# Reordering the preparation of a bidirectional RWKV-7 scan inside a hybrid encoder kernel

## The reference

```
h = rms_norm(x); P = h @ w_in        # columns: RWKV-7 | convolution | latent attention | gates
RWKV-7:  p = p + (0.5*(prev + next) - p) * mu
         decay = exp(-exp(-softplus(-(w0 + tanh(wd) @ w_up)) - 0.5))      # per direction
         icl   = sigmoid(a0 + ad @ a_up)                                  # per direction
         v     = v + (v_first - v) * sigmoid(v0 + (h @ v_down) @ v_up)    # second layer only
         kk    = normalized(k * k_k) per head;  k_dir = k * (1 + (icl - 1) * k_a)
         state = state * w_t + (state a_t) b_t^T + v_t k_t^T;  out_t = state r_t   # both directions
         o = layer_norm(out + reversed out); o += bonus(r, k_dir, v); y = (o * g) @ w_branch
conv:    u = val * sigmoid(gate); 31-tap depthwise convolution; silu(layer_norm(u)) @ w_branch
merge:   x += (sum over branches of sigmoid(gate_b) * y_b) @ w_o
```

## Time and profile before

| | |
|---|---|
| median of 3 runs | 1811.07 us (1809.88 to 1813.27) |
| profiled execution | 1806.79 us, of which the span from first to last instruction is 1805.1 us |
| mean granted PE clock | 0.946 |
| PE busy | 1633.4 us, 90% |
| DVE busy | 1235.8 us, 68% |
| ACT busy | 769.1 us, 43% |
| POOL busy | 92.4 us, 5% |
| DMA | 231.58 MB, mean 128 GB/s |

### The profile page before, as it was taken

How to read it: one execution, slowest core, us unless ns; L and a number is a source line. 1 busy time by engine, 2 the same in 40 slices (tenths; PEclk the granted TensorE clock), 3 DMA queues, 4 the chain that set the end, 5 groups by cost and what they waited for, 6 DMA issues and landing times.

```text
span 1805.1 us, 43648 instructions
## 1 busy us (share of the span) xinstructions
PE 1633.4 (90%) x17117; PEld 1507.3 (84%) x17117; DVE 1235.8 (68%) x1850; ACT 769.1 (43%) x1163; POOL 92.4 (5%) x112
## 2 busy tenths in 40 slices
PE   6999998868878889999999999988688788999999
PEld 6999986757868869999889988867588687899997
DVE  5677667897647556777666777678874665567766
ACT  5444553435232135544444446534342311355444
POOL 1000100001100001000000002000011000010000
PEclk9999998978979989999999999989689799999999
DMA  5755532222102025555556554222220121355555
GB/s 187 263 181 184 173 106 71 94 94 71 38 25 84 27 81 165 178 187 178 189 195 227 187 185 166 94 71 95 70 85 25 36 72 38 102 165 180 187 183 192
DMA packets 62927, 231.58 MB, mean 128 GB/s; under 512 B 7024, under 2 KB 8048, under 8 KB 61840
## 3 DMA queue, kind: packets, MB, share of 16 engines
q1 hardware_dynamic: 61488, 221.41, 36.4%
q0 software_dynamic: 1248, 7.46, 1.1%
HBM read 228.09 MB, written 1.05 MB: 127 GB/s over the span
## 4 chain that ended last, share of the span: by engine, by line
PE 70%; DVE 14%; issue 9%; ACT 5%; DMA 2%; DVEq 0%; ACTq 0%; SPq 0%; POOLq 0%
PE banks L538 14%; PE banks L540 13%; PE banks L539 13%; PE banks L605 9%; PE banks L606 5%; DVE wlo L1407 3%; PE banks L939 2%; DMA raw<-in_stream 2%; DVE cvx L1635 2%; PE banks L937 2%; PE banks L928 1%; PE banks L865 1%; ACT whi L1083 1%; DVE arena L1848 1%; ACT arena L1260 1%
## 5 line engine op out<-in xcount | busy, mean ns | idle before, releaser
L1407 DVE TENSOR_TENSOR wlo<-raw,whi 128x1024 fp32r<-128x1024 f32 x417 | 511.8, 1231 | 327.0 <-ACT whi L1083 325.8
L1083 ACT CAST whi<-raw 128x1024 fp32r<-128x1024 f32 x417 | 435.4, 1048 | 442.4 <-PE banks L540 296.7
L538 PE MATMUL banks<-hx,whi 128*128 128x256 f32 x1696 | 491.9, 290 | 52.5 <-DVE wlo L1407 19.5
L540 PE MATMUL banks<-hx,wlo 128*128 128x256 f32 x1696 | 486.8, 287 | 0.0
L539 PE MATMUL banks<-hx,whi 128*128 128x256 f32 x1696 | 486.7, 287 | 0.0
L538 PEld LDWEIGHTS banks<-hx,whi 128*128 128x128 f32 x1696 | 332.6, 196 | 58.9 <-issue 20.6
L539 PEld LDWEIGHTS banks<-hx,whi 128*128 128x128 f32 x1696 | 332.6, 196 | 0.2
L540 PEld LDWEIGHTS banks<-hx,wlo 128*128 128x128 f32 x1696 | 332.3, 196 | 0.0
L538 PE MATMUL banks<-h,whi 128*128 128x256 f32 x896 | 275.1, 307 | 29.4 <-ACT arena L1180 16.6
L539 PE MATMUL banks<-h,whi 128*128 128x256 f32 x896 | 263.6, 294 | 0.0
L540 PE MATMUL banks<-h,wlo 128*128 128x256 f32 x896 | 262.9, 293 | 0.0
(11 more groups left out here) (293 smaller groups left out, 1888.8 us busy)
## 6 DMA issues: line engine op xcount, KB each, us to landing
raw<-in_stream SPq DMA_DIRECT2D x417, 512.0 KB, 3.3
arena<-in_wuq POOLq DMA_DIRECT2D x2, 1152.0 KB, 11.0
lo_w<-in_lora POOLq DMA_DIRECT2D x2, 1024.0 KB, 7.6
arena<-in_wukv POOLq DMA_DIRECT2D x2, 1024.0 KB, 15.0
xT<-in_x SPq DMA_DIRECT2D x1, 1024.0 KB, 4.9
out<-xT SPq DMA_DIRECT2D x8, 128.0 KB, 3.5
consts<-in_cst SPq DMA_DIRECT2D x1, 642.5 KB, 8.4
vec_t<-in_vecs POOLq DMA_DIRECT2D x3, 113.0 KB, 4.1
```

What stands on the lines that cost most here:

```text
L538: TE.matmul(o, wh, hi, start=first, stop=False, **kw)
L540: return TE.matmul(o, wl, hi, start=False, stop=last, **kw)
L1083: SE.copy(whi[:, m % HL, :], raw[:, m % RAW, :]).then_inc(hi_ready, 1)
L1407: TT(wlo[:, m % HL, :], raw[:, m % RAW, :], whi[:, m % HL, :].bitcast(F), ALU.subtract)\
```

## The change

The change has these parts, in both layers:

1. Column mixing: ACT writes a second copy of each column, scaled by 1 - mu, beside the plain one; DVE then needs two instructions for a column and not three. Two tiny DVE instructions a layer make the scale vectors.
2. The key's squares are taken by ACT straight from k with scale k_k, ahead of the last attention output. The multiplication by k_k on DVE goes; it is done in one instruction with the spread inverse norm.
3. First preparation: key sums, then at once the low-rank products for decay and icl, then the value gate, then the spread inverse norm. DVE does the prefix sums first and kk and the values after; the b and k products come before the exponentials' results are used. The three kinds of turned copies wait each for its own input.
4. Of the taps, 4 instead of 3 come after each attention pair; the other 42 go into the first solve, 4 in each of the five levels and 22 behind them. The convolution's mean and variance go behind the first solve, and its tail (sigmoid, products, rounding) into the second direction.
5. The update of `vfirst` goes into the second direction's solve.
6. States: only the three chunks that are needed are computed, each in one bank of its own; the step from state to state is accumulated by PE on top of the local state, and one DVE instruction over 128 partitions takes the place of four over 64. The added outputs take two banks and two DVE additions in place of four.
7. The second direction's low-rank products, sigmoids, prefix sums and b and k products go into the first direction's state steps.
8. `FILL_R` is redistributed; its sum stays 192.

The core of the diff:

```diff
-FILL_R = {"key sums": 8, "key inverse": 8, "values": 8}
+FILL_R = {"key sums": 6, "decay": 8, "nu": 5, "values": 5}
 for _d in range(2):
-    FILL_R.update({("lora", _d): (14, 8)[_d], ("kr", _d): (36, 26)[_d], ("tk", _d): (5, 6)[_d], ("pairs", _d, 0): 9,
+    FILL_R.update({("kr", _d): (14, 16)[_d], ("tk", _d): (4, 6)[_d], ("pairs", _d, 0): (6, 20)[_d],
...
+            all_members = [m for i in range(2) for q in QUADS for m in members(q)[i::2]]
+            def local(d, i):
+                c, b = STATE_ORDER[d][i], bank[STATE_BANKS[i]]
+                t, e = c // 2, slice(HD * (c % 2), HD * (c % 2) + HD)
+                for n, (x, h, r, j) in enumerate(all_members):
...
+                    TE.matmul(b[r:r + HD, j * HD:(j + 1) * HD], tk[e, 2, t, hs], vt[e, t, hs], start=n < 2, stop=False,
+                              skip_group_check=True)
...
+                if d == 0:
+                    pe.wait_ge(*act.at("key squares"))
...
+                    fr.at("key sums")
+                    pe.wait_ge(*act.at("wag"))
+                    lora(0, 0, (0, 1))
+                    lora(0, 1, (2, 3))
+                    fr.at("decay")
...
+                    m.then_inc(*ten.mark("nu"))
+                    fr.at("nu")
...
+                    m.then_inc(*ten.mark("key spread"))
+                    fr.at("values")
+                    pe.wait_ge(*vec.at("values"))
...
+                fr.at(("kr", d))
+                pe.wait_ge(*vec.at(("kr kk", d)))
...
                 for i in range(3):
+                    if i:
+                        pe.wait_ge(*vec.at(("bt" if i == 1 else "kt", d)))
...
+                local(d, 1)
+                if d == 0:
+                    pe.wait_ge(*vec.at(("conv", *CONV_TAPS[-1][::-1])))
...
                 fr.at(("o", d))
+                local(d, 0)
...
+                local(d, 2)
+                if d == 0:
+                    lora(1, 0, (1, 4))
...
+                    if d == 0 and i == 1:
+                        pe.wait_ge(*act.at(("sw", 1)))
+                        lora(1, 1, (1, 4))
...
@@ ACT
-                        SE.copy(pp[:, i % 4, 1:S + 1], src[:, 0:S]).then_inc(*act.mark(("column", n)))
+                        SE.copy(pp[:, i % 4, 1:S + 1], src[:, 0:S])
+                        SE.mul(pt[:, i % 4, :], src[:, 0:S], mus[:, 0, i:i + 1]).then_inc(*act.mark(("column", n)))
...
                 fr.at(("tk", d))
-                for q in QUADS:
-                    fr.at(("pairs", d, q))
-                if d == 0:
+                if d:
                     for c in range(RC):
                         sc.wait_ge(*poo.at(("cv normed", c)))
...
+                for q in QUADS:
+                    fr.at(("pairs", d, q))
...
@@ DVE
-                conv(3)
+                conv(4)
...
+                        conv(4)
+                    elif lv == 1:
+                        TT(v_diff, v_, vfirst[:, :, :], ALU.subtract).then_inc(*vec.mark("first difference"))
...
+                if d == 0:
+                    conv(len(taps))
                 fr.at(("x", d))
...
                 for i in (1, 2):
...
+                    TT(qw[:, :, chunks[i], :], state(i, 0), decay(i), ALU.mult).then_inc(*vec.mark(("qw", d, i)))
                     fr.at(("state", d, i))
+                    if d == 0 and i == 1:
+                        decays(1)
+                if d == 0:
+                    directed(1)
+                    ve.wait_ge(*act.at("cv rms"))
```

More of the change, by code:

```diff
@@ L827, in _ @@
             pe.wait_ge(*vec.at(("u", 2, RC - 1)))
-            fr.at("key sums")
-            pe.wait_ge(*act.at("key squares"))
-            for j in range(RC):
-                m = TE.matmul(bank[4][0:H, 0:S], cc("es", H, j * SUMS), tA[:, j, :], start=j == 0, stop=j == RC - 1)
-            m.then_inc(*ten.mark("key sums"))
-            fr.at("key inverse")
-            pe.wait_ge(*act.at(("column", T_VD)))
-            pe.wait_ge(lora_in, L * 16 + 16)
-            for c in range(RC):
-                m = TE.matmul(bank[c // 2][:, (c % 2) * S:(c % 2 + 1) * S], lo_w[0:32, 3, c * P:(c + 1) * P],
-                              wag[0:32, 3, :], start=True, stop=True)
@@ L839, in _ @@
-            m.then_inc(*ten.mark("nu"))
-            pe.wait_ge(*vec.at("key inverse"))
-            for j in range(RC):
-                for e in range(2):
-                    m = TE.matmul(bank[2 + j // 2][HD * e:HD * e + HD, (j % 2) * S:(j % 2 + 1) * S],
-                                  picked(2 * j + e, HD), rn_rw[0:H, 0, :], start=True, stop=True)
-            m.then_inc(*ten.mark("key spread"))
-            fr.at("values")
-            pe.wait_ge(*vec.at("values"))
-            pe.wait_ge(*act.at("key rms"))
@@ L1280, in _ @@
                 fa.at(("turned pair", p), 1)
+                if p == PAIRS - 1:
+                    for c in range(RC):
+                        sc.wait_ge(*vec.at(("mixed", RC + c)))
+                        m = SE.activation(tA[:, c, :], k_[:, c, :], ACT.Square, scale=vv("k_k", c))
+                    m.then_inc(*act.mark("key squares"))
                 u_round(p)
@@ L1295, in _ @@
             SE.preload_act_table(ACT.Sigmoid)
-            fr.at("key inverse")
-            sc.wait_ge(*ten.at("nu"))
-            for c in range(RC):
-                m = SE.activation(tB[:, c, :], bank[c // 2][:, (c % 2) * S:(c % 2 + 1) * S], ACT.Sigmoid,
-                                  bias=vv("v0", c))
-            m.then_inc(*act.mark("nu"))
-            fr.at("values")
-            sc.wait_ge(*ten.at("vt"))
-            for t in range(NT):
-                m = SE.copy(vt[:, t, :], bank[4 + t][:, :])
@@ L1323, in _ @@
                 m.then_inc(*act.mark(("icl", d)))
+            for d in range(2):
+                if d == 0:
+                    sw(0, (0, 1))
+                    icl(0, (2, 3))
+                    fr.at("decay")
+                    sc.wait_ge(*ten.at("nu"))
+                    for c in range(RC):
+                        m = SE.activation(nu[:, c, :], bank[4 + c // 2][:, (c % 2) * S:(c % 2 + 1) * S], ACT.Sigmoid,
+                                          bias=vv("v0", c))
+                    m.then_inc(*act.mark("nu"))
+                    SE.activation(wag[:, 2, :], wag[:, 2, :], ACT.Sigmoid).then_inc(*act.mark("wag gate"))
+                    fr.at("nu")
@@ L1762, in _, with decays @@
             by_tile = lambda a: a.rearrange("p c (t q) -> p c t q", t=NT)
-            for d in range(2):
+            def decays(d):
                 ve.wait_ge(*act.at(("sw", d)))
-                if d == 0:
-                    ve.wait_ge(*vec.at("first values"))
                 for c in range(RC):
@@ new lines, in _ @@
+                state = lambda i, at: bank[STATE_BANKS[i]][:, at:at + S].rearrange("p (j n) -> p j n", j=RC)
+                decay = lambda i: wch[:, :, chunks[i]].unsqueeze(2).broadcast_to([P, RC, HD])
+                ve.wait_ge(*ten.at(("local", d, 0)))
+                ve.wait_ge(*vec.at(("wch", d)))
+                TT(qw[:, :, chunks[0], :], state(0, 0), decay(0), ALU.mult).then_inc(*vec.mark(("qw", d, 0)))
+                for i in (1, 2):
+                    ve.wait_ge(*ten.at(("local", d, i)))
+                    TT(ptr[:, :, chunks[i], :], one.unsqueeze(1).broadcast_to([P, RC, C]), state(i, S), ALU.subtract)\
+                        .then_inc(*vec.mark(("ptr", d, i)))
```

341 lines of the change are left out of this document (158 added, 183 removed).

## The result

The changed kernel takes 1738.5 us (median of 4 runs, 1736.28 to 1741.63) against 1810.5 us before (4 runs), a ratio of 0.961 with a 95% interval of 0.9584 to 0.9631. The forecast was 1736. The profiled execution took 1740.1 us, its span 1738.1 us: 67.0 us less span than before, where the forecast had 74.6.

What follows compares the result with a forecast made beforehand. PE was taken as the bound (busy 90%), with time won where it waits or runs at lower clock. Terms sum to -37.3 us a layer, -74.6 for two: 1806.8 to 1732.2, plus 4.3 gives 1736 us; range 1706 to 1773.

Steps and rivals of the forecast that it cites:

- First preparation: Last attention piece to first pair product: 72.0 us becomes 34.3, a loss of 37.7 us a layer, bounds -30 to -41.
- The 2 us of clock: First preparation: the forecast 4.1 us wait for the values brings back some half clock, costing 2 us a layer.
- the 1.3 us that the forecast had PE wait for kk: End of the first preparation: PE waits about 1.3 us for DVE's kk, besides 4.1 us for the values.
- Attention: Attention stage: DVE loses 15 instructions of 426 ns and gains 4 taps; net -3 us a layer, bounds -6 to +2.
- First solve to the second pairs: From the first solve to the second pair product: 110.4 us before, loses 24.2 us a layer, bounds -17 to -28.
- the 0.9 us of the pairs: First direction's pairs: 5 pieces less, but DVE's masks then bind, so -0.9 us a layer.
- Second pairs: Second direction's pairs: 22 more pieces and a 7.1 us wait for POOL's convolution tail; +12.4 us a layer, bounds +4 to +18.
- the one us a layer that the prediction named and left out of its sum: Second pairs: masks' additions with two SBUF inputs contend with POOL and lengthen the convolution's tail, about one us a layer.
- States: Second direction's states: 38 more pieces, 13.6 us, less 6.4 us given back; +7.2 us a layer, bounds +3 to +12.
- Clock: Forecast waits of 4.1, 2.1 and 7.1 us bring half clock: 2 + 2 + 4 = 8 us a layer, bounds 3 to 16.
- the tail was not in time: Rival, second pairs: convolution's tail is in time; its wait, clock and late mask go, 12 us a layer, 1712 us; 12%.
- DVE was not late in the levels: Rival, first solve and its states: taps aren't covered and DVE is late, 17 us a layer, 1770 us; 17%.
- half clock ended with the pairs: Rival "Slower": half clock after the 7.1 us wait stays through the second direction, 81 us a layer, 1898 us; 5%.

Runs made afterwards that it cites:

- experiment 1: Changed kernel with the 42 remaining taps back in DVE's first preparation and none in the solve; 1763.4 us, ratio 0.9748 to the kernel before.
- experiment 5: Changed kernel with column mixing as before, three DVE instructions per column and no scaled ACT copy; 1741.1 us, ratio 0.9618 to the kernel before.
- experiment 3: experiment 2 with the end of the convolution's preparation on ACT and POOL also left out; 1707.8 us, ratio 0.9449 to the kernel before.
- experiment 4: Changed kernel with the second direction's preparation behind the first direction's states instead of between their steps; 1738.4 us, ratio 0.9612 to the kernel before.
- experiment 2: Changed kernel with the convolution's branch product fed from the attention's rounded input, so PE needn't wait for POOL; 1714.5 us, ratio 0.9473 to the kernel before.
- experiment 10: Changed kernel run again, unaltered; 1731.5 us, ratio 0.9574 to the kernel before.

## Why the prediction was right, step by step

- **First preparation.** 34.3 us by hand, 34.4 measured, its wait 3.77 for 4.1. Experiment 1 shows the reason: put back, the taps make DVE the bound again, 14.5 us a layer. The text said that 37 pieces leave this stage; it was 29. The other 8 stood ahead of it, in the attention's stage by its windows. Of the 37.6 us that the stage lost, the taps are 14.5 (experiment 1), the 29 pieces 10.3 and the statistics 3.8 as forecast; the other 9 us are the new order of the products and the clock, which no kernel takes back alone. The forecast's bound of -30 allowed for DVE's instructions slower beside PE's and ACT's traffic; no row shows that, and DVE's products over 128x1024 kept their 1.22 us here. The 2 us of clock did not add: the 14 pieces behind the wait took 6.6 us for 5.0 at full clock, but that went into the 1.3 us that the forecast had PE wait for kk, and no such wait was left.
- **Attention.** -3 forecast, -5.7 measured, and by another cause. The term credited the mixing, which experiment 5 shows to be worth nothing there. The gain is the 8 pieces, which the sum had added to the second direction without taking them off here, and the 2.24 us wait ahead of them.
- **First solve to the second pairs.** -24.2 and 2 of clock forecast, -18.5 measured. From the first pair product to the first level it was 12.5 us before and is 11.3 now, so the 0.9 us of the pairs came. They were lost again in the levels, which were at 0.95 (32.4 us for 31.4). Taps hidden: right (experiment 1). The part behind the levels was built as 37.3 us and took 41.9. Of the 4.6 us, half clock takes up to 0.04 x 41.9 = 1.7 us, an issue gap (PE idle with nothing in the profile that it waits for) ahead of a local state 1.24 us, and GpSimd beside DVE 1.1 us (experiment 3). That the preparation may lie beside the states was worth only 1.6 us (experiment 4). By the windows the 18.7 us that this part lost are 10.2 us of busy PE (18 pieces are 6.4 of them; the clock went from 0.80 to 0.96) and 8.5 us of idle PE. Among the waits that went are those of the earlier trace rows and one in a state step, in PE's timeline of before:

```profile
517.17 0.68 PE L1016 MATMUL banks<-arena 64*64 64x64 f32 x16 [2.79 <-DVE arena L1891]
```

  No kernel takes the new state step back by itself, so its share is read from the traces and not shown by a run.
- **Second pairs.** +12.4 and 4 of clock forecast, +17.7 measured. The new wait was 8.34 us for 7.1: POOL's last four subtractions took 3.75 us, not 2.78, beside DVE's additions in SBUF: the one us a layer that the prediction named and left out of its sum. Experiment 2 puts the wait's whole price at 10.9 us a layer.
- **States.** +7.2 forecast, +11.7 measured, inside its bound of 12. This is the largest mis-sized term, and the traces place it. The 38 pieces are 13.5 us as forecast, so the stage gave back 1.8 us, not 6.4. The state steps' two waits of 1.14 us went. The products of unused chunks gave back nothing: before, 192 products of the chunks took 3.5 us, now 128 take 4.1 us. PE's timelines of before and after:

```profile
619.71 0.30 PE L1002 MATMUL banks<-arena 64*64 64x64 f32 x8
619.82 0.30 PE L998 MATMUL banks<-arena 64*64 64x64 f32 x8
```

```profile
585.56 0.63 PE L855 MATMUL banks<-arena 64*64 64x64 f32 x16
586.02 0.63 PE L851 MATMUL banks<-arena 64*64 64x64 f32 x16
```

  8 products start every 0.12 us before, 16 every 0.46 us now: 0.015 and 0.029 us for each. In the old order the two halves of the input rows (`e`) take turns; in the new one a local state uses one half throughout. That this is the reason is not shown by a run. An issue gap of 1.61 us ahead of the local states (1.20 before) and the wait of 3.64 us for the bonus terms (4.01 before) stayed.
- **Clock.** 8 us a layer forecast. From the windows at most (1 - clock) x length was lost: 1.7 in the preparation, 3.7 in the next stage, 5.0 in the pairs, 0.7 in the states; part of that is idle time.

By layer the errors are -2.7 (attention), -1.0 ahead of it, -1.9 (preparation and clock), +3.7, +1.3, +0.7 (levels) and +4.5, in sum +4.6 of the -37.3. The second layer repeats it: the same wait stands 860 us later. The median came out 2.5 us above the forecast and not some 8, since it lay below its profiled run while before it lay above. So part of the hit is luck of the runs, and part is errors that cancel: +10.2 us a layer in four terms against -5.6 in three, of which the attention's -2.7 has another cause than the one forecast. All rivals failed: the tail was not in time, DVE was not late in the levels, and half clock ended with the pairs.

## What to carry to other kernels

Before moving filler work into a wait, list who frees its buffers: here the filler's merges stood in another engine's list in steps of eight, and both attempts to fill a wait by moving pieces (12 into one of 8.3 us, 6 into one of 3.8 us) made new waits of 5 to 9 us. Starting the awaited chain earlier and interleaving it per chunk gave 3.4 us a layer in its place. Work goes for nothing into idle time that repeats in a short cycle (1.19 and 0.65 us in each level, for 1.66 us of taps), if it is read from the rows of the instructions behind it; and the price of taking work off a chain is found by putting it back alone. Leaving products out saves PE time only if the rest keep their rate: here 64 fewer took 0.6 us more.

## What the runs showed of the hardware

- **Half clock strikes the same program in different places.** Two profiles of the changed kernel, windows of the same levels of the first layer (that of experiment 10 is with experiment 1 above):

```profile
415.30:447.80 32.50, 29.79 (x897) 28.96 (x899) 25.13 (x40) 0.00 (x0) 0.00 (x0) 0.95 0.02 5
```

  32.5 us at 0.95 and 30.5 at 1.00, with the same instructions. The stretch from the outputs to the second pairs differs as much, 40.4 at 0.96 and 38.7 at 1.00; the first preparation does not (34.4 and 34.3). Such differences of 2 us are larger than several effects that were looked for, so stages are to be compared at equal clock.
- **GpSimd slows some of DVE's instructions and not others.** Beside POOL's two-input products, DVE's products with both inputs in SBUF went from 1.22 to 1.75 us, a copy of 128x16 from 0.17 to 0.70 us. A mask whose first input is a bank kept its time, in DVE's timeline beside POOL's last products and subtractions (499.8 to 506.5):

```profile
500.22 1.22 DVE L1849 TENSOR_TENSOR arena<-banks,masks 128x1024 f32<-128x1024 f32 x1
502.19 1.63 DVE L1859 TENSOR_TENSOR arena<-arena,consts 128x1024 f32<-128x1024 f32 x1
```

  The Trainium skill, "SBUF — State Buffer", section "Who interferes with whom", says that a VectorE instruction with two SBUF inputs contends with a GpSimd one that reads SBUF, that copies can contend too, and that the later one waits until the other is done. Which instructions are slowed agrees with the rows here. The price was 0.4 to 0.5 us on each of DVE's, and POOL's four products there took 5.75 us, 1.44 each for 0.70.
